# Where the last three columns of the recurrent mixer are taken out of PSUM, and what the bonus sums wait for

## The chip, the cores and the metric

The kernel runs on one core of a Trainium2 chip. The metric is the device time of one launch in microseconds (us). TensorE (PE in the profile) multiplies, VectorE (DVE), ScalarE (ACT) and GpSimd (POOL) work elementwise, SyncE (SP) issues DMAs.

## The reference

The reference is one step of a two-layer decoder trunk over 256 prompt tokens and 8 sequences of 8 sample tokens (320 columns in all). The change sits in the third branch of the mixer, RWKV-7 time mixing:

```
mixed = rwkv_cols + (prev - rwkv_cols) * mu          # token shift over 26 x 128 projected rows
r, kc, vc, wd, ad, gd = split(mixed)
decay = exp(-exp(w_log));  a_lr = sigmoid(a0 + ad @ w_a2)
kk = kc * k_k;  kc = kc * (1 + (a_lr - 1) * k_a);  kk = kk / |kk|
yr, state = rwkv7_scan(r, decay, kc, vc, kk, kk * a_lr, state)
bonus = sum_head(r * kc * r_k) * vc
out_c = (head_norm(yr) * lnx_g + lnx_b + bonus) * g_rw
```

## The kernel before

All activations lie transposed, 128 features by 320 tokens. A weight matrix comes in chunks of 128 by 1024, one for each 128 outputs, and each chunk makes one tile of 128 by 320 in PSUM. For accuracy a chunk is split in a high half (ACT, line 1531) and a low half (POOL line 732 here, DVE line 1944 elsewhere), so TensorE multiplies a chunk in 24 matmuls: 16 with the high half, then 8 with the low half (lines 897, 898 and 901 for the columns of the mixer). SP loads the chunks into a ring of four; a load waits until the chunk four places ahead is multiplied. Four PSUM tiles, gemm_banks, take the results in turn.

The recurrent mixer of a layer runs in four steps.

1. **Columns.** 26 chunks, `rwkv`, numbered c = 0 to 25. DVE takes each tile out of PSUM in `mix_tokens` (lines 2065 to 2070, five instructions) into `mixed`, in the order of ORDER; from then the bank is free (semaphore `psum_free`). Behind that, `prepare_rwkv(c)` does a share of the elementwise preparation of the scan: products of whole tensors of 128x2560 and the eight bonus products r * r_k * kc (128x320 each, line 2117), written into E3, with the mark "rk" behind the eighth. Its last product, kk * a_lr, has the mark "mixed".
2. **Filling chunks.** 15 chunks of `fill_rwkv`, projections that other branches need later, whose results ACT copies to a stage buffer (line 1604) and SP stores to memory. They give TensorE work while DVE ends the preparation. Chunk 0 and 1 go into banks 2 and 3 and wait for 24 columns out of PSUM; chunk 2 and those behind it wait for all 26 and for the filling chunk two before. On TensorE they are lines 946, 947 (high) and 951 (low).
3. **Bonus sums.** Behind four filling chunks, `tile_sums` (line 1016, 10 matmuls of 128x512) sums E3 over each head into mixer_banks and the first tile of gemm_banks. It waits for "rk" and "mixed". Eleven filling chunks follow. DVE waits for the sums (mark "rks"), multiplies them with v (lines 2134 and 2135), sets a state to zero with the mark "done", and scales r and the gate (lines 2149, 2151).
4. **Scan.** It starts on TensorE (line 1052) behind the fifteenth filling chunk and "done".

POOL, in its own order, makes the low halves of the 26 columns and the first four filling chunks, waits for "mixed", issues the store of the shifted columns `sh_out` (line 762), and then makes the low halves of the next 13 chunks, each behind the wait for its high half and for the chunk two before.

Each engine runs its own list in the order written; every DVE instruction of this part is followed by a wait for its own end (`V_`). The marks are semaphores that count up in the order of `pre_v`.

```
if c < 2: pe.wait_ge(psum_free, RING + BASE["rwkv"] + RT - 2)
else:     pe.wait_ge(psum_free, RING + pos - 1)
```

Of the kernel before, what the change touches and what calls it, by code (L numbers as in the profile page):

```python
# [33 lines left out]
KT = D // P  # L34
L = 2
TP = 256
# [11 lines left out]
C64 = 64  # L48
# [46 lines left out]
PREP_FILLS = 15  # L95
XSCALE = float(D // NX) ** -0.5
# [251 lines left out]
def build(nc, ins, outs):  # L348

    with ExitStack() as ctx:  # L350
# [371 lines left out]
        def _(pool):  # L722
# [20 lines left out]
            with pool.Fori(0, L) as l:  # L743
# [17 lines left out]
                pool.wait_ge(pre_v.sem, pre_v.value["mixed"])  # L761
# [106 lines left out]
        def _(pe):  # L868
# [119 lines left out]
            def need(m, name):  # L988
                pe.wait_ge(m.sem, m.value[name])
# [48 lines left out]
            def rwkv():  # L1038
                fill("fill_rwkv", 4)
                need(pre_v, "rk")  # L1040
                need(pre_v, "mixed")
# [880 lines left out]
        def _(dve):  # L1922
# [173 lines left out]
            def prepare_rwkv(c):  # L2096

                (b0, b1), (r0_, r1_), (v0, v1) = sum_spans(), spans(rr), spans(vv)
# [16 lines left out]
                if c == 22:  # L2115
                    for i in range(KT):
                        ins_ = stt(E3[:, i], rr[:, i], PR("r_k", i), kk_[:, i], ALU.mult, ALU.mult)
                        V_(ins_) if i < KT - 1 else V_.mark(ins_, pre_v, "rk")
                if c == 23:
                    ar0, kkc, ec = AR[:, :, 0:NCH, 0], chunks64(Bt[:, :, 0:TP]), chunks64(E[:, :, 0:TP])  # L2120
                    V_(tt(ar0[:, :, :, 1:C64], kkc[:, :, :, 1:C64], ec[:, :, :, 0:C64 - 1], ALU.mult))
                    V_(copy(ar0[:, :, :, 0], kkc[:, :, :, 0]))
                    V_(copy(pend, ec[:, :, :, C64 - 1]))
                if c == 24:
                    ar0 = AR[:, :, NCH, 0].rearrange("p a (b t) -> p a b t", t=SL)
                    kkc, ec = (v[:, :, TP:T].rearrange("p a (b t) -> p a b t", t=SL) for v in (Bt, E))
                    V_(tt(ar0[:, :, :, 1:SL], kkc[:, :, :, 1:SL], ec[:, :, :, 0:SL - 1], ALU.mult))
                    V_(copy(ar0[:, :, :, 0], kkc[:, :, :, 0]))
                    V_(copy(pends, ec[:, :, :, SL - 1]))
                    V_(tt(kk_, kk_, LW, ALU.mult))  # L2130
                if c == RT - 1:
                    V_.mark(tt(Bt, Bt, Aa, ALU.mult), pre_v, "mixed")
                    need(pre_p, "rks")
                    V_(tt(r0_, b0, v0, ALU.mult))
                    V_.mark(tt(r1_, b1, v1, ALU.mult), pre_v, "bonus")
                    arrived(dve, layer, "x_stored")
                    arrived(dve, layer, "shift_stored")
# [557 lines left out]
```

## Time and profile before

| | us |
|---|---|
| runs of the kernel | 3093.7, 3097.57, 3096.59 (median 3096.59) |
| profiled execution: span from first to last instruction | 3101.2 |
| profiled execution: time of its own beside the span | not listed |
| TensorE busy | 2848.1 |
| VectorE busy | 1749.0 |
| ScalarE busy | 1255.2 |
| GpSimd busy | 521.7 |
| mean granted TensorE clock, share of full | 0.955 |

The span is a time of one execution, 4.6 us above the median of the three runs. Busy time says how long an engine was executing, over stages whose limits differ. The timeline of an engine gives, for each instruction, its start, its duration and the idle time ahead of it with what ended it. "x8" after a row means that eight like it follow one another and that the duration is that of all eight. On TensorE the start of the next matmul comes before the end of the last one, since they are pipelined.

### The profile page before, as it was taken

What the parts mean: (1) busy time and instruction counts of PE and PEld (TensorE: products, weight loads), DVE (VectorE), ACT (ScalarE), POOL (GpSimd) and SP (SyncE); (2) the same over time, 40 slices, a digit from 0 to 9 for tenths busy, and PEclk for the clock granted to TensorE, in tenths of its full rate; (3) what the DMA queues carried; (4) which work ended last, traced back from release to release, by engine and by line L of the source; (5) the groups of instructions that cost most, each with busy time, mean ns of one, the idle gap of its engine ahead of it and who ended that gap; (6) DMA issues with size and microseconds to landing.
All of it is one profiled execution on the core that took longest, in us unless ns stands there. A gap on an engine that the chain in (4) does not pass through costs nothing. (4 is left out here: it accounts for less than half of the span.)

```text
span 3101.2 us, 63944 instructions
## 1 busy us (share of the span) xinstructions
PE 2848.1 (92%) x25694; PEld 2651.8 (86%) x25694; DVE 1749.0 (56%) x2611; ACT 1255.2 (40%) x1755; POOL 521.7 (17%) x341
## 2 busy tenths in 40 slices
PE   7998989989989999899989988999798899998997
PEld 7998888877788998799989978987787888977997
DVE  4444764586676665544354457545766766655443
ACT  4534631244332443444254355222543234434542
POOL 0003550054310000000000046400543000000000
PEclk9999989999998999899999999999999999999998
DMA  4444350144374566344344443401454664663443
GB/s 160 150 147 145 109 152 18 29 124 172 98 300 144 180 209 220 130 149 148 116 148 149 147 136 114 130 25 30 127 188 124 251 214 142 220 220 113 149 147 105
DMA packets 119694, 448.21 MB, mean 145 GB/s; under 512 B 13648, under 2 KB 23920, under 8 KB 111664
## 3 DMA queue, kind: packets, MB, share of 16 engines
q1 hardware_dynamic: 97920, 329.78, 33.4%
q0 software_dynamic: 21552, 115.34, 10.1%
q8 instruction: 156, 2.56, 0.3%
q14 instruction: 66, 0.54, 0.1%
HBM read 397.04 MB, written 48.02 MB: 144 GB/s over the span
## 5 line engine op out<-in xcount | busy, mean ns | idle before, releaser
L1531 ACT ACTIVATE w_high<-ring 128x1024 fp32r<-128x1024 f32 x598 | 631.9, 1057 | 746.9 <-PE gemm_banks L901 315.7
L897 PE MATMUL gemm_banks<-in_high,w_high 128*128 128x320 f32 (+1 forms) x2720 | 803.3, 311 | 25.5 <-ACT w_high L1531 13.9
L1944 DVE TENSOR_TENSOR w_low<-ring,w_high 128x1024 fp32r<-128x1024 f32 x436 | 532.5, 1222 | 472.7 <-ACT w_high L1531 472.3
L898 PE MATMUL gemm_banks<-in_low,w_high 128*128 128x320 f32 (+1 forms) x2720 | 795.4, 308 | 0.0
L732 POOL TENSOR_TENSOR w_low<-ring,w_high 128x1024 fp32r<-128x1024 f32 x162 | 414.3, 2566 | 970.9 <-ACT w_high L1531 969.7
L897 PEld LDWEIGHTS gemm_banks<-in_high,w_high 128*128 128x128 f32 x2720 | 515.1, 189 | 32.4 <-issue 14.0
L898 PEld LDWEIGHTS gemm_banks<-in_low,w_high 128*128 128x128 f32 x2720 | 514.9, 189 | 1.7
L901 PE MATMUL gemm_banks<-in_high,w_low 128*128 128x320 f32 (+1 forms) x2720 | 450.8, 308 | 6.3 <-POOL w_low L732 3.8
L901 PEld LDWEIGHTS gemm_banks<-in_high,w_low 128*128 128x128 f32 x2720 | 408.8, 189 | 8.7 <-POOL w_low L732 5.3
L946 PE MATMUL gemm_banks<-in_high,w_high 128*128 128x320 f32 x640 | 208.9, 339 | 22.1 <-DVE arena L2070 16.7
L973 PE MATMUL gemm_banks<-act_high,w_high 128*128 128x320 f32 x704 | 208.2, 308 | 2.5 <-DVE arena L1993 2.5
L974 PE MATMUL gemm_banks<-act_low,w_high 128*128 128x320 f32 x704 | 207.9, 310 | 0.0
L947 PE MATMUL gemm_banks<-in_low,w_high 128*128 128x320 f32 x640 | 199.5, 324 | 0.0
L885 PE MATMUL gemm_banks<-in_high,w_high 128*128 128x320 f32 (+1 forms) x592 | 128.4, 348 | 58.3 <-ACT in_high L1547 53.8
L885 PEld LDWEIGHTS gemm_banks<-in_high,w_high 128*128 128x128 f32 x592 | 97.5, 205 | 84.2 <-issue 45.9
L946 PEld LDWEIGHTS gemm_banks<-in_high,w_high 128*128 128x128 f32 x640 | 128.6, 201 | 43.5 <-issue 31.6
L1604 ACT ACTIVATE stage<-gemm_banks 128x320 f32<-128x320 f32 x80 | 35.0, 437 | 273.4 <-PE gemm_banks L951 255.5
L1052 PE MATMUL gemm_banks<-arena 64*64 64x64 f32 (+1 forms) x2976 | 121.4, 223 | 17.1 <-DVE arena L2172 10.7
L973 PEld LDWEIGHTS gemm_banks<-act_high,w_high 128*128 128x128 f32 x704 | 131.7, 187 | 3.6 <-DVE arena L1993 3.6
L974 PEld LDWEIGHTS gemm_banks<-act_low,w_high 128*128 128x128 f32 x704 | 133.1, 189 | 0.0
L947 PEld LDWEIGHTS gemm_banks<-in_low,w_high 128*128 128x128 f32 x640 | 129.1, 202 | 2.9 <-issue 2.9
L1052 PEld LDWEIGHTS gemm_banks<-arena 64*64 64x64 f32 x2976 | 105.7, 135 | 22.8 <-ACT arena L1726 8.2
(420 smaller groups left out, 4237.4 us busy)
## 6 DMA issues: line engine op xcount, KB each, us to landing
ring<-in_w SPq DMA_DIRECT2D x598, 512.0 KB, 3.6
arena<-in_kc POOLq DMA_DIRECT2D x14, 1024.0 KB, 6.5
arena<-in_vc POOLq DMA_DIRECT2D x14, 1024.0 KB, 7.3
out_fill<-stage SPq DMA_DIRECT2D x80, 160.0 KB, 4.0
arena<-in_ssm POOLq DMA_DIRECT2D x16, 512.0 KB, 13.5
out_s_ssm<-arena POOLq DMA_DIRECT2D x16, 512.0 KB, 13.9
arena<-in_ret POOLq DMA_DIRECT2D x16, 512.0 KB, 22.2
out_s_ret<-arena POOLq DMA_DIRECT2D x16, 512.0 KB, 7.0
```

The costliest lines, as they stand in the source:

```text
L732: nc.gpsimd.tensor_tensor(w_low[:, slot], ring[:, pos % RING, 0:D], w_high[:, slot].bitcast(F32), ALU.subtract).then_inc(weights_split, 1)
L885: mm(dst, w_high[:, slot, w(k)], in_high[:, k, 0:n], start=(k == 0), stop=False)
L897: mm(dst, w_high[:, slot, w(k)], in_high[:, k, 0:n], start=(k == 0), stop=False)
L898: mm(dst, w_high[:, slot, w(k)], in_low[:, k, 0:n], start=False, stop=False)
L901: ins_ = mm(dst, w_low[:, slot, w(k)], in_high[:, k, 0:n], start=False, stop=(k == KT - 1))
L946: mm(dst, w_high[:, slot, w], in_high[:, k], start=(k == 0), stop=False)
L947: mm(dst, w_high[:, slot, w], in_low[:, k], start=False, stop=False)
L973: mm(dst, w_high[:, slot, w], act_high[:, k], start=(k == 0), stop=False)
L974: mm(dst, w_high[:, slot, w], act_low[:, k], start=False, stop=False)
L1052: ins_ = mm(dst[r_], w[r_], src[r_], start=start, stop=stop, skip_group_check=not start)
L1531: f(w_high[:, slot], ring[:, s, 0:D], ACT.Copy).then_inc(weights_high, 1)
L1944: tt(w_low[:, slot], ring[:, pos % RING, 0:D], w_high[:, slot].bitcast(F32), ALU.subtract).then_inc(weights_split, 1)
```

## The change

The eight bonus products are spread over four columns by a table, BONUS_AT: two behind column 22, one behind 23, one behind 24, four behind 25. The products and copies that stood behind columns 23 and 24, and the one behind column 25, go into a new function, `products_rwkv`, which runs behind column 25 and its bonus products. TensorE no longer waits for "mixed" ahead of the bonus sums, only for "rk"; POOL waits for "rk" in the place of "mixed" ahead of the store of `sh_out`. The order of instructions on PE, ACT, POOL and SP stays; only DVE's changes. The names of the marks stay in one order. Line numbers behind line 95 shift by up to 3.

```diff
--- before.py
+++ after.py
@@ -93,6 +93,7 @@
 TOKQ = [0, 1, 8, 7]
 SAVES = 7 + 3 * NS
 PREP_FILLS = 15
+BONUS_AT = {22: (0, 1), 23: (2,), 24: (3,), 25: (4, 5, 6, 7)}
 XSCALE = float(D // NX) ** -0.5
 gate_base = {"ffa13": 0, "ffa2": 0, "ffb13": FT, "ffb2": FT}
 
@@ -758,7 +759,7 @@
                 fill("rwkv", RT // 2, RT)
 
                 fill("fill_rwkv", 0, AHEAD + 2)
-                pool.wait_ge(pre_v.sem, pre_v.value["mixed"])
+                pool.wait_ge(pre_v.sem, pre_v.value["rk"])
                 pool.dma_start(outs["shift"][l], sh_out).then_inc(dma["shift_stored"][0], 16)
                 fill("fill_rwkv", AHEAD + 2, PREP_FILLS + AHEAD)
                 for c in range(NCH):
@@ -1038,7 +1039,6 @@
             def rwkv():
                 fill("fill_rwkv", 4)
                 need(pre_v, "rk")
-                need(pre_v, "mixed")
                 tile_sums(pre_p, "rks", K("bones"), E3)
                 fill("fill_rwkv", PREP_FILLS - 4)
                 need(pre_v, "done")
@@ -2095,7 +2095,6 @@
 
             def prepare_rwkv(c):
 
-                (b0, b1), (r0_, r1_), (v0, v1) = sum_spans(), spans(rr), spans(vv)
                 if c in (16, 18):
                     half = (c - 16) // 2
                     need(pre_p, ("kkss", half))
@@ -2112,29 +2111,31 @@
                 if c == 21:
                     need(pre_a, "norms")
                     V_(tt(Bt, Bt, E3, ALU.mult))
-                if c == 22:
-                    for i in range(KT):
-                        ins_ = stt(E3[:, i], rr[:, i], PR("r_k", i), kk_[:, i], ALU.mult, ALU.mult)
-                        V_(ins_) if i < KT - 1 else V_.mark(ins_, pre_v, "rk")
-                if c == 23:
-                    ar0, kkc, ec = AR[:, :, 0:NCH, 0], chunks64(Bt[:, :, 0:TP]), chunks64(E[:, :, 0:TP])
-                    V_(tt(ar0[:, :, :, 1:C64], kkc[:, :, :, 1:C64], ec[:, :, :, 0:C64 - 1], ALU.mult))
-                    V_(copy(ar0[:, :, :, 0], kkc[:, :, :, 0]))
-                    V_(copy(pend, ec[:, :, :, C64 - 1]))
-                if c == 24:
-                    ar0 = AR[:, :, NCH, 0].rearrange("p a (b t) -> p a b t", t=SL)
-                    kkc, ec = (v[:, :, TP:T].rearrange("p a (b t) -> p a b t", t=SL) for v in (Bt, E))
-                    V_(tt(ar0[:, :, :, 1:SL], kkc[:, :, :, 1:SL], ec[:, :, :, 0:SL - 1], ALU.mult))
-                    V_(copy(ar0[:, :, :, 0], kkc[:, :, :, 0]))
-                    V_(copy(pends, ec[:, :, :, SL - 1]))
-                    V_(tt(kk_, kk_, LW, ALU.mult))
+                for i in BONUS_AT.get(c, ()):
+                    ins_ = stt(E3[:, i], rr[:, i], PR("r_k", i), kk_[:, i], ALU.mult, ALU.mult)
+                    V_(ins_) if i < KT - 1 else V_.mark(ins_, pre_v, "rk")
                 if c == RT - 1:
-                    V_.mark(tt(Bt, Bt, Aa, ALU.mult), pre_v, "mixed")
-                    need(pre_p, "rks")
-                    V_(tt(r0_, b0, v0, ALU.mult))
-                    V_.mark(tt(r1_, b1, v1, ALU.mult), pre_v, "bonus")
-                    arrived(dve, layer, "x_stored")
-                    arrived(dve, layer, "shift_stored")
+                    products_rwkv()
+
+            def products_rwkv():
+
+                (b0, b1), (r0_, r1_), (v0, v1) = sum_spans(), spans(rr), spans(vv)
+                ar0, kkc, ec = AR[:, :, 0:NCH, 0], chunks64(Bt[:, :, 0:TP]), chunks64(E[:, :, 0:TP])
+                V_(tt(ar0[:, :, :, 1:C64], kkc[:, :, :, 1:C64], ec[:, :, :, 0:C64 - 1], ALU.mult))
+                V_(copy(ar0[:, :, :, 0], kkc[:, :, :, 0]))
+                V_(copy(pend, ec[:, :, :, C64 - 1]))
+                ar0 = AR[:, :, NCH, 0].rearrange("p a (b t) -> p a b t", t=SL)
+                kkc, ec = (v[:, :, TP:T].rearrange("p a (b t) -> p a b t", t=SL) for v in (Bt, E))
+                V_(tt(ar0[:, :, :, 1:SL], kkc[:, :, :, 1:SL], ec[:, :, :, 0:SL - 1], ALU.mult))
+                V_(copy(ar0[:, :, :, 0], kkc[:, :, :, 0]))
+                V_(copy(pends, ec[:, :, :, SL - 1]))
+                V_(tt(kk_, kk_, LW, ALU.mult))
+                V_.mark(tt(Bt, Bt, Aa, ALU.mult), pre_v, "mixed")
+                need(pre_p, "rks")
+                V_(tt(r0_, b0, v0, ALU.mult))
+                V_.mark(tt(r1_, b1, v1, ALU.mult), pre_v, "bonus")
+                arrived(dve, layer, "x_stored")
+                arrived(dve, layer, "shift_stored")
 
             def strided(v, *dims, skip=0):
                 return bass.AP(tensor=v.tensor, offset=v.offset + skip, ap=[list(v.ap[0])] + [list(d) for d in dims])
```

DVE behind column 22, before. The row of line 2117 is the bonus products (E3); lines 2065 to 2070 take column 23 out of PSUM; 2121 and 2122 make the first part of AR from Bt and E.

```order
L2117 SCALAR_TENSOR_TENSOR arena<-arena,par 128x320 x8
L2065 TENSOR_SCALAR arena<-gemm_banks,omu 128x320
L2066 SCALAR_TENSOR_TENSOR arena<-gemm_banks,par,arena 128x255
L2068 SCALAR_TENSOR_TENSOR arena<-gemm_banks,par,arena 128x8x7
L2069 SCALAR_TENSOR_TENSOR arena<-gemm_banks,omu,arena 128x8
L2070 TENSOR_SCALAR arena<-gemm_banks 128x9
L2121 TENSOR_TENSOR arena<-arena 128x8x4x63
L2122 COPY arena<-arena 128x8x4
L2123 COPY chunk_decay<-arena 128x32
```

And in the changed kernel, from the same place:

```order
L2115 SCALAR_TENSOR_TENSOR arena<-arena,par 128x320 x2
L2065 TENSOR_SCALAR arena<-gemm_banks,omu 128x320
L2066 SCALAR_TENSOR_TENSOR arena<-gemm_banks,par,arena 128x255
L2068 SCALAR_TENSOR_TENSOR arena<-gemm_banks,par,arena 128x8x7
L2069 SCALAR_TENSOR_TENSOR arena<-gemm_banks,omu,arena 128x8
L2070 TENSOR_SCALAR arena<-gemm_banks 128x9
L2115 SCALAR_TENSOR_TENSOR arena<-arena,par 128x320
```

Two bonus products stand ahead of column 23 in the place of eight, and one behind it where line 2121 and two copies stood.

DVE from the end of column 24 to the bonus, before. Lines 2127 to 2130 are the products of the sample tokens and kk_ * LW, 2132 is Bt * Aa (mark "mixed"), 2134 the product with the bonus sums.

```order
L2070 TENSOR_SCALAR arena<-gemm_banks 128x9
L2127 TENSOR_TENSOR arena<-arena 128x8x8x7
L2128 COPY arena<-arena 128x8x8
L2129 COPY chunk_decay<-arena 128x64
L2130 TENSOR_TENSOR arena<-arena 128x2560
L2065 TENSOR_SCALAR arena<-gemm_banks,omu 128x320
L2066 SCALAR_TENSOR_TENSOR arena<-gemm_banks,par,arena 128x255
L2068 SCALAR_TENSOR_TENSOR arena<-gemm_banks,par,arena 128x8x7
L2069 SCALAR_TENSOR_TENSOR arena<-gemm_banks,omu,arena 128x8
L2070 TENSOR_SCALAR arena<-gemm_banks 128x9
L2132 TENSOR_TENSOR arena<-arena 128x2560
L2134 TENSOR_TENSOR arena<-mixer_banks,arena 128x2048
```

In the changed kernel, from the end of column 25 (its last instruction is the first row):

```order
L2070 TENSOR_SCALAR arena<-gemm_banks 128x9
L2115 SCALAR_TENSOR_TENSOR arena<-arena,par 128x320 x4
L2124 TENSOR_TENSOR arena<-arena 128x8x4x63
L2125 COPY arena<-arena 128x8x4
L2126 COPY chunk_decay<-arena 128x32
L2129 TENSOR_TENSOR arena<-arena 128x8x8x7
L2130 COPY arena<-arena 128x8x8
L2131 COPY chunk_decay<-arena 128x64
L2132 TENSOR_TENSOR arena<-arena 128x2560
L2133 TENSOR_TENSOR arena<-arena 128x2560
L2135 TENSOR_TENSOR arena<-mixer_banks,arena 128x2048
```

All three groups of wide products stand behind column 25 and the last four bonus products, next to one another.

## Rows read from the trace of the kernel before

**Rows 1.** The page: span, and the busy row of TensorE (us, share).
```profile
span 3101.2 us, 63944 instructions
PE 2848.1 (92%) x25694; PEld 2651.8 (86%) x25694; DVE 1749.0 (56%) x2611; ACT 1255.2 (40%) x1755; POOL 521.7 (17%) x341
```

**Rows 2.** Timeline, PE, layer 1: start, us; in brackets idle before and releaser.
```profile
376.85 1.44 PE L901 MATMUL gemm_banks<-in_high,w_low 128*128 128x320 f32 x8 [1.13 <-POOL w_low L732]
...
384.00 1.34 PE L901 MATMUL gemm_banks<-in_high,w_low 128*128 128x320 f32 x8
387.34 0.38 PE L946 MATMUL gemm_banks<-in_high,w_high 128*128 128x320 f32 x1 [2.01 <-DVE arena L2070]
...
402.48 0.61 PE L946 MATMUL gemm_banks<-in_high,w_high 128*128 128x320 f32 x1 [6.33 <-DVE arena L2070]
...
412.33 3.59 PE L1016 MATMUL mixer_banks<-arena,const 128*128 128x512 f32 x8
...
418.96 1.34 PE L951 MATMUL gemm_banks<-in_high,w_low 128*128 128x320 f32 x8
...
454.16 1.34 PE L951 MATMUL gemm_banks<-in_high,w_low 128*128 128x320 f32 x8
```

**Rows 3.** Timeline, PE, layer 2, same columns.
```profile
1920.36 1.33 PE L901 MATMUL gemm_banks<-in_high,w_low 128*128 128x320 f32 x8
...
1938.85 0.60 PE L946 MATMUL gemm_banks<-in_high,w_high 128*128 128x320 f32 x1 [6.33 <-DVE arena L2070]
...
1955.15 1.34 PE L951 MATMUL gemm_banks<-in_high,w_low 128*128 128x320 f32 x8
```

**Rows 4.** Windows, layer 1: length, busy (PE, PEld, DVE, ACT, POOL), PEclk, DMA, GB/s.
```profile
340.00:368.00 28.00, 25.73 (x160) 23.78 (x158) 21.66 (x35) 18.20 (x12) 15.67 (x6) 1.00 0.37 122
...
388.00:390.00 2.00, 2.00 (x10) 2.00 (x9) 2.00 (x1) 0.79 (x1) 0.99 (x1) 0.51 0.96 356
404.00:406.00 2.00, 2.00 (x9) 2.00 (x9) 1.25 (x1) 0.00 (x0) 0.03 (x1) 0.50 0.69 207
```

**Rows 5.** Timeline, DVE, layer 1, from the bonus products to the end of preparation.
```profile
376.36 8.95 DVE L2117 SCALAR_TENSOR_TENSOR arena<-arena,par 128x320 f32<-128x320 f32 x8
...
387.11 4.00 DVE L2121 TENSOR_TENSOR arena<-arena 128x2016 f32<-128x2016 f32 x1
391.14 2.29 DVE L2122 COPY arena<-arena 128x32 f32<-128x32 f32 x1
...
397.29 0.22 DVE L2129 COPY chunk_decay<-arena 128x64 f32<-128x64 f32 x1
...
400.40 0.55 DVE L2065 TENSOR_SCALAR arena<-gemm_banks,omu 128x320 f32<-128x320 f32 x1
...
402.16 0.17 DVE L2070 TENSOR_SCALAR arena<-gemm_banks 128x9 f32<-128x9 f32 x1
402.25 3.01 DVE L2132 TENSOR_TENSOR arena<-arena 128x2560 f32<-128x2560 f32 x1
416.89 2.29 DVE L2134 TENSOR_TENSOR arena<-mixer_banks,arena 128x2048 f32<-128x2048 f32 x1 [11.63 <-PE gemm_banks L1016]
...
439.92 2.19 DVE L2152 MEMSET arena<- 128x2560 f32 x1 [0.60 <-DVE arena L2151]
```

**Rows 6.** Timeline, ACT, layer 1: high halves of the first two filling chunks.
```profile
385.50 1.06 ACT L1531 ACTIVATE w_high<-ring 128x1024 fp32r<-128x1024 f32 x1 [7.07 <-DMA ring<-in_w]
389.21 1.06 ACT L1531 ACTIVATE w_high<-ring 128x1024 fp32r<-128x1024 f32 x1 [2.66 <-DMA ring<-in_w]
```

**Rows 7.** Timeline, POOL, layer 1: low halves beside the columns and filling chunks.
```profile
390.35 3.02 POOL L732 TENSOR_TENSOR w_low<-ring,w_high 128x1024 fp32r<-128x1024 f32 x1 [1.35 <-ACT w_high L1531]
394.12 2.40 POOL L732 TENSOR_TENSOR w_low<-ring,w_high 128x1024 fp32r<-128x1024 f32 x1 [0.76 <-ACT w_high L1531]
397.64 4.93 POOL L732 TENSOR_TENSOR w_low<-ring,w_high 128x1024 fp32r<-128x1024 f32 x1 [1.12 <-ACT w_high L1531]
...
421.79 2.49 POOL L732 TENSOR_TENSOR w_low<-ring,w_high 128x1024 fp32r<-128x1024 f32 x1 [5.47 <-ACT w_high L1531]
```


## The prediction

> **What bounds the kernel now.** I read the page first: TensorE is busy 92% of the span [rows 1], so the time is TensorE's work plus the places where it stands still or runs at the lower clock. Then the waits of TensorE by length: the longest one in the mixer's preparation is the first matmul of a filling chunk behind DVE's line 2070, the last instruction that takes a column out of PSUM. Then the timelines of TensorE, DVE, ACT and POOL around it, and the granted clock by windows.
>
> TensorE's timeline [rows 2] is to be read from the low part of the last column (start 384.00) to the low part of the fifth filling chunk (start 418.96): 34.96 us. What must lie between is five chunks and the bonus sums. A chunk costs 3.52 us: the tenth chunk behind the one of 418.96 starts its low part at 454.16, and 35.20 / 10 = 3.52. Of these, the 16 high matmuls are 3.52 - 1.18 = 2.34 us, as the eight low ones start 1.34 - 0.16 = 1.18 us before the next. The bonus sums start at 412.33 and the high part behind them at 418.96 - 2.34 = 416.62, so they cost 4.29 us. Five chunks and the sums are 17.60 + 4.29 = 21.89 us. The stretch loses **13.07 us**. In layer 2 the same two rows are 1920.36 and 1955.15, 34.79 us apart [rows 3]: a loss of **12.90 us**.
>
> The loss has three parts. The first filling chunk waits 2.01 us for column 23 to leave PSUM, the third waits 6.33 us for column 25 [rows 2], and the rest, 13.07 - 8.34 = 4.73 us, is clock: behind each of the two waits the granted clock is 0.51 and 0.50 of full, the 1.2 GHz level [rows 4].
>
> Why is column 25 late? DVE does the eight bonus products in front of column 23 (8.95 us) and wide products in front of columns 24 and 25; its last instruction for column 25 ends at 402.16 + 0.17 = 402.33 [rows 5]. TensorE had finished that column at 384.00 + 1.34 = 385.34 [rows 2].
>
> **The change, part by part, layer 1.**
>
> *Order on DVE.* The same instructions run, so DVE's own sum is unchanged; what counts is which are in front. Column 23 now has two bonus products in front of it, which start at 376.36 [rows 5]. At the mean of the row, 8.95 / 8 = 1.12 us each, they end at 378.6; if both are among the long ones, some 2 us later. Column 23 was finished at 376.85 + 1.44 = 378.29 [rows 2] and takes 1.85 us to leave PSUM (five instructions, for column 25 from 400.40 to 402.25 [rows 5]). So it is out by 380.5 to 383. Columns 24 and 25 follow as TensorE ends them: column 25 is out at 385.34 + 1.85 = 387.2 in place of 402.3, in the bad case near 390. Either is before the third filling chunk can start, and the 6.33 us go, with the clock that they cost.
>
> *First filling chunk.* What is late next is its own high half: ACT starts it at 385.50 for 1.06 us, behind the weights' DMA [rows 6]. It can start at 386.56, so 1.22 us of 2.01 stay.
>
> *Second filling chunk.* The first ends its matmuls at 386.56 + 3.52 = 390.08, and the second's high half is there at 389.21 + 1.06 = 390.27 [rows 6]: 0.19 us. Its low half took POOL from 390.35 to 393.37 [rows 7] and is wanted at 390.27 + 2.34 = 392.61: 0.76 us.
>
> *Third to sixth.* DVE's wide products now stand beside these chunks without columns between. A low half takes POOL 2.40 or 2.49 us [rows 7] at its usual pace, but 4.93 us in the row of 397.64, which lies over line 2130. The usual low half starts at 421.79, 1.65 us behind the end of the fifth chunk (418.96 + 1.18 = 420.14), and is wanted at 420.14 + 3.52 + 2.34 = 426.00, 4.21 us after its start. At 2.49 us it costs nothing; at 4.93 us TensorE waits 0.72 us. Bounds for the four chunks are 0 and 4 x 0.72 = 2.9 us; I take one such wait, 0.7, because only one of the four low halves of this kind before (390.35, 394.12, 397.64 and the usual one) was that long.
>
> The Trainium skill, "SBUF — State Buffer", section on the two sides of SBUF, says that a GpSimd operation and a DVE operation with two SBUF inputs hold a port pair in turn, each for its whole instruction. By it the worst low half would be one wide product and itself, 3.01 + 2.40 = 5.4 us, and the wait 1.2 us in place of 0.72. The trace agrees in kind: a copy of 128x32 took 2.29 us and one of 128x64 took 0.22 us [rows 5].
>
> *The waits for "mixed".* TensorE now wants only "rk" in front of the sums. "rk" comes at 387.2 + 4 x 1.12 = 391.7 (395 at worst); TensorE reaches the sums at about 402. POOL passes its wait before the low half of the fifth filling chunk, so nothing queued there is held; the store of `sh_out` starts earlier and blocks nothing.
>
> *DVE behind the sums.* From 387.11 to 402.25 + 3.01 = 405.26 DVE was at the wide products and at columns 24 and 25 without a break [rows 5]; 18.15 less 2 x 1.85 us leaves 14.4 us for the wide products, with their contention. They run from 391.7 to about 406.1. The sums now end near 406.5, so DVE starts line 2134 as soon as before relative to TensorE. It needed from 416.89 to 439.92 + 2.19 = 442.1 for all that the scan wants [rows 5], and TensorE is there at 454.16 + 1.18 = 455.3: 13 us of cover stay. If this cover were gone, the scan would start later by what is missing.
>
> **Sum.** Left over in layer 1: 1.22 + 0.19 + 0.76 + 0.7 = 2.9 us. Gained: 13.07 - 2.9 = 10.2 us; layer 2 by the same steps 12.90 - 2.9 = 10.0. Behind the scan's start all is tied to TensorE, so it reaches the end. Against the profiled execution: 3101.2 - 20.2 = 3081.0 us of span. The median of the runs shown lies 4.6 us under that span, so the runs should give 3096.6 - 20.2 = **3076.4 us**.
>
> Bounds of the known case: with only 1.22 + 0.19 left over, 11.6 a layer, 3073.4. With four long waits and the clock at its lower level for one more chunk (below: 2.97 us) and through the first, which adds about 0.65 as it overlaps the wait for the second's low half: 2.17 + 2.9 + 2.97 + 0.65 = 8.7 left, 4.3 gained a layer, 3088. Some 2 us of scatter between runs come on top.
>
> **Rivals.**
>
> *The clock does not come back in full.* Idle times of 1.22, 0.76 and 0.7 us remain within ten us. For it: an idle time of 2.01 was followed by 0.51 [rows 4]. Against: the window 340 to 368 has 28.00 - 25.73 = 2.3 us idle and a clock of 1.00 [rows 4], and the 1.13 us at 376.85 were followed by chunks at full pace. A chunk at the lower level is 408.97 - 402.48 = 6.49 us (to the end of the third, 412.33 + 0.16 - 3.52), 2.97 too many. One or two such chunks a layer leave a gain of 4.3 to 7 us a layer: about 3085 us.
>
> *Slower: POOL and DVE take turns, and the clock stays low.* Place: filling chunks 2 to 8, where the wide products and then lines 2134 to 2152 run beside POOL. If each low half takes 4.93 us, TensorE waits 0.72 us in every chunk, and if the clock falls for these chunks too, each costs 3.69 us. From the third such chunk this eats the 10.2 us. With five: 18.5 - 10.9 (the gain without the wait already counted) = 7.6 us a layer, 3096.6 + 15 = 3112 us. Against it: DVE worked beside POOL from 416.89 to 442.1 before, with a low half of 2.49 us in it [rows 7] and TensorE at 3.52 us a chunk from 418.96 on.
>
> The Trainium skill, "TensorE: Matmul & The Clock Gate", section on PSUM-queue depth-cycling, has a case for it: frequent small idle times between groups of matmuls made the clock swing between its two levels. The trace shows 2.3 us of such idle time from 340 to 368 without a lower clock, so I give it little.
>
> *The gain is taken back at the scan.* If DVE ended its preparation more than 13 us later relative to TensorE, "done" or the zeroed arrays would hold the scan, and the time would be 3094 to 3097. For it: DVE's work is dense from 385 on. Against: the sum above has it on time, with 13 us of cover. The same time would come out if the third chunk were held by something else than `psum_free`; but its low half was ready at 394.12 + 2.40 = 396.5 [rows 7], six us before it was used.
>
> **How the numbers follow.** Forecast 0.76, clock rival 0.13, taken back 0.07, slower 0.04. About 0.2% (6.2 us) is what a measurement of this kernel can tell from no change. Forecast and clock rival are faster by more: 0.89. Taken back is within: 0.07. The predicted time is the likeliest, 3076.4. The range goes from 3071.5 (the upper bound of the gain with scatter) to 3087 (the clock rival and most of the lower bound); it leaves out the last two cases and little of the first.
>
> **What would show it.** Right: the idle time of 6.33 us in front of line 946 gone in both layers; the third filling chunk starting within 10 us of the last column's end (17 before); the clock near 1.00 from 394 on; low part to low part as above 24 to 25 us; "DVE waits for the sums" shorter by about as much as the wide products moved; one or two short waits of line 951 for POOL. Wrong: a clock of 0.5 in that stretch, low halves of 5 us in a row, or an idle TensorE in front of the scan's first matmul.

## The result, and the profile after

| | before | changed |
|---|---|---|
| median of the runs measured side by side, us (six each) | 3096.3 | 3082.18 |
| lowest and highest | 3093.7 to 3099.06 | 3062.27 to 3087.43 |
| profiled execution, span | 3101.2 | 3082.2 |
| profiled execution, its own time | not listed | 3083.83 |
| mean granted clock | 0.955 | 0.958 |

The medians differ by 14.1 us. The ratio of the two kernels' times is given as 0.9943, which is 17.6 us of 3096.3, with a 95% interval of 0.9921 to 0.9965, or 10.8 to 24.5 us: faster, and clear of no change. The forecast was 3076.4 us (20.2 us faster), the range 3071.5 to 3087. The two profiled executions differ by 19.0 us of span.

TensorE's timeline of the changed kernel, layer 1, by start and duration; it answers to [rows 2].

```profile
377.06 1.44 PE L902 MATMUL gemm_banks<-in_high,w_low 128*128 128x320 f32 x8 [1.14 <-POOL w_low L733]
...
384.20 1.34 PE L902 MATMUL gemm_banks<-in_high,w_low 128*128 128x320 f32 x8
386.69 0.41 PE L947 MATMUL gemm_banks<-in_high,w_high 128*128 128x320 f32 x1 [1.16 <-ACT w_high L1531]
...
389.17 1.43 PE L952 MATMUL gemm_banks<-in_high,w_low 128*128 128x320 f32 x8
391.65 0.41 PE L947 MATMUL gemm_banks<-in_high,w_high 128*128 128x320 f32 x1 [1.05 <-ACT w_high L1531]
...
395.79 1.44 PE L952 MATMUL gemm_banks<-in_high,w_low 128*128 128x320 f32 x8 [1.53 <-POOL w_low L733]
397.07 0.31 PE L947 MATMUL gemm_banks<-in_high,w_high 128*128 128x320 f32 x1
...
407.55 1.02 PE L1017 MATMUL gemm_banks<-arena,const 128*128 128x512 f32 x2
410.75 1.33 PE L952 MATMUL gemm_banks<-in_high,w_low 128*128 128x320 f32 x8
...
447.21 0.27 PE L1052 MATMUL mixer_banks<-arena 64*64 64x64 f32 x2
```

The idle time of 6.33 us is gone, and that of 2.01 us has become 1.16. From low part (384.20) to low part (410.75) it is 26.55 us, against 34.96 before: 8.41 us gained. In layer 2 the same rows start at 1914.52 and 1941.08:

```profile
1914.52 1.34 PE L902 MATMUL gemm_banks<-in_high,w_low 128*128 128x320 f32 x8
1917.04 0.42 PE L947 MATMUL gemm_banks<-in_high,w_high 128*128 128x320 f32 x1 [1.18 <-ACT w_high L1531]
...
1921.63 0.41 PE L947 MATMUL gemm_banks<-in_high,w_high 128*128 128x320 f32 x1 [0.68 <-ACT w_high L1531]
...
1926.13 1.44 PE L952 MATMUL gemm_banks<-in_high,w_low 128*128 128x320 f32 x8 [1.89 <-POOL w_low L733]
...
1941.08 1.34 PE L952 MATMUL gemm_banks<-in_high,w_low 128*128 128x320 f32 x8
```

26.56 us, against 34.79: 8.23 gained. Windows of layer 1, with the granted clock in the column behind the five busy times (they answer to [rows 4], columns as there):

```profile
388.00:390.00 2.00, 2.00 (x14) 1.86 (x14) 1.96 (x2) 0.00 (x0) 1.12 (x1) 1.00 0.94 369
394.00:396.00 2.00, 0.47 (x3) 0.21 (x2) 1.97 (x2) 0.00 (x0) 2.00 (x2) 1.00 0.31 121
404.00:408.00 4.00, 4.00 (x12) 1.84 (x12) 3.97 (x2) 1.38 (x2) 4.00 (x2) 1.00 0.77 237
```

The clock is 1.00 where it was 0.51 and 0.50, even in the window that holds the longest idle time left. DVE's timeline of the same stretch answers to [rows 5]:

```profile
387.40 0.17 DVE L2070 TENSOR_SCALAR arena<-gemm_banks 128x9 f32<-128x9 f32 x1
387.48 3.75 DVE L2115 SCALAR_TENSOR_TENSOR arena<-arena,par 128x320 f32<-128x320 f32 x4
391.26 2.26 DVE L2124 TENSOR_TENSOR arena<-arena 128x2016 f32<-128x2016 f32 x1
393.56 2.24 DVE L2125 COPY arena<-arena 128x32 f32<-128x32 f32 x1
395.83 2.31 DVE L2126 COPY chunk_decay<-arena 128x32 f32<-128x32 f32 x1
...
398.84 2.40 DVE L2130 COPY arena<-arena 128x64 f32<-128x64 f32 x1
401.27 0.22 DVE L2131 COPY chunk_decay<-arena 128x64 f32<-128x64 f32 x1
401.52 2.83 DVE L2132 TENSOR_TENSOR arena<-arena 128x2560 f32<-128x2560 f32 x1
404.38 4.86 DVE L2133 TENSOR_TENSOR arena<-arena 128x2560 f32<-128x2560 f32 x1
409.28 2.29 DVE L2135 TENSOR_TENSOR arena<-mixer_banks,arena 128x2048 f32<-128x2048 f32 x1
...
434.80 2.19 DVE L2153 MEMSET arena<- 128x2560 f32 x1 [0.60 <-DVE arena L2152]
448.55 0.42 DVE L2165 TENSOR_TENSOR arena<-mixer_banks,const 128x256 f32<-128x256 f32 x1 [11.55 <-PE mixer_banks L1059]
```

Column 25 is out at 387.57 in place of 402.33. Before line 2135 DVE no longer idles (11.63 us before): the wide products end at 409.24, 0.7 us behind the bonus sums (407.55 + 1.02 = 408.57). ACT's timeline has the high half of the second filling chunk, which answers to the second row of [rows 6]:

```profile
390.54 1.06 ACT L1531 ACTIVATE w_high<-ring 128x1024 fp32r<-128x1024 f32 x1 [3.90 <-DMA ring<-in_w]
```

Last, POOL's timeline, which answers to [rows 7]; the third row is the store of `sh_out`:

```profile
391.68 6.42 POOL L733 TENSOR_TENSOR w_low<-ring,w_high 128x1024 fp32r<-128x1024 f32 x2 [2.56 <-ACT w_high L1531]
398.74 2.41 POOL L733 TENSOR_TENSOR w_low<-ring,w_high 128x1024 fp32r<-128x1024 f32 x1 [0.64 <-ACT w_high L1531]
401.09 0.56 POOL L763 DMA_DIRECT2D out_shift<-arena  x1
402.27 9.26 POOL L733 TENSOR_TENSOR w_low<-ring,w_high 128x1024 fp32r<-128x1024 f32 x2 [0.61 <-ACT w_high L1531]
```

Two low halves in 6.42 us, then two in 9.26 us, where two alone take 4.8. The first of these holds TensorE for 1.53 us; the second pair lies beside the bonus sums, and no wait of TensorE follows it.

### The profile page after: what moved, and what is told of

It reads as the page before. It is cut to its first block and busy times, and to the rows that moved or that the text cites. A ratio compares the mean times of both kernels' runs of the same rounds, so it can differ in the third digit from the quotient of the medians.

```text
span 3082.2 us, 63942 instructions
## 1 busy us (share of the span) xinstructions
PE 2840.6 (92%) x25694; PEld 2642.0 (86%) x25694; DVE 1760.4 (57%) x2611; ACT 1255.6 (41%) x1755; POOL 527.6 (17%) x341
## 5 line engine op out<-in xcount | busy, mean ns | idle before, releaser
L1052 PEld LDWEIGHTS gemm_banks<-arena 64*64 64x64 f32 x2976 | 106.3, 136 | 24.5 <-ACT arena L1726 8.3
## 6 DMA issues: line engine op xcount, KB each, us to landing
out_s_ssm<-arena POOLq DMA_DIRECT2D x16, 512.0 KB, 14.1
```

The costliest lines, as they stand in the source:

```text
L1052: ins_ = mm(dst[r_], w[r_], src[r_], start=start, stop=stop, skip_group_check=not start)
```

## The experiments

**Theory.** What brought the gain is that columns 23 to 25 leave PSUM ahead of the wide products: TensorE stands still less, and it keeps its clock. What lacks to the forecast lies in the first two filling chunks: their loads, and POOL's turn behind line 2124. **Rivals.** The gain comes from the dropped waits for "mixed", and returns to 6.3 us of idle time once they are back; or the difference to the forecast is the scatter of the granted clock elsewhere in the program.

The totals scatter by more than most of these edits are worth, so each kernel is read in two ways: by its total, and by a stretch of its profile, from the first matmul of the last column's low part to the first matmul of the scan. It holds all that the change touches:

| kernel | stretch, layer 1 / layer 2, us | of it at 1.2 GHz | total, median (runs) | ratio to before, 95% |
|---|---|---|---|---|
| before | 71.4 / 71.3 | 13.7 / 10.2 | | |
| changed | 63.0 / 63.0 | 0 / 0 | 3082.2 (6) | 0.9921 to 0.9965 |
| e1, both waits back | 66.3 / 66.5 | 3.4 / 3.4 | 3089.6 (5) | 0.9939 to 0.9982 |
| e2, POOL's wait back | 64.9 / 63.4 | 3.4 / 0 | 3080.1 (4) | 0.9887 to 0.9946 |
| e3, waits alone dropped | 73.2 / 73.2 | 10.2 / 10.2 | 3094.2 (7) | 0.9959 to 0.9993 |
| e4, changed again | 63.1 / 63.1 | 0 / 0 | 3077.0 (4) | 0.9911 to 0.9947 |
| e5, bonus early | 62.1 / 62.2 | 3.4 / 3.4 | 3077.6 (6) | 0.9913 to 0.9962 |
| e6, bonus late | 60.4 / 60.2 | 0 / 0 | 3072.9 (8) | 0.9902 to 0.9948 |
| e7, a low half on DVE | 61.1 / 61.0 | 0 / 0 | 3077.8 (6) | 0.9898 to 0.9967 |
| e8, e7 and loads earlier | 59.2 / 59.2 | 0 / 0 | 3078.3 (6) | 0.9925 to 0.9974 |
| e9, before, TensorE kept busy | 68.7 / 73.3 | 3.4 / 6.8 | 3088.9 (10) | 0.995 to 0.9989 |
| e10, loads earlier | 58.6 / 58.6 | 0 / 0 | 3079.3 (6) | 0.9927 to 0.9968 |
| e11, loads earlier, bonus late | 58.4 / 58.4 | 0 / 0 | 3077.8 (9) | 0.9917 to 0.996 |
| e12, changed, a third time | 63.1 / 61.8 | 0 / 0 | 3082.1 (10) | 0.9932 to 0.9968 |

One more run of e1 took 6958.75 us; why is not known, and it is not counted here (with it the median is 3090.9). Each stretch comes from one profile, so it is one execution's. The changed kernel has three profiles: five of its six stretches are 63.0 or 63.1 us, the sixth 61.8. The kernel before has one, and the part on the waits shows that its stretch can be some 2 us longer.

### The waits

e1 puts both waits for "mixed" back into the changed kernel, e2 POOL's alone, e3 drops TensorE's alone from the kernel before.

```diff
 # e1
-                pool.wait_ge(pre_v.sem, pre_v.value["rk"])
+                pool.wait_ge(pre_v.sem, pre_v.value["mixed"])
...
                 need(pre_v, "rk")
+                need(pre_v, "mixed")
```

> The changed kernel with both waits for mixed put back (TensorE ahead of the bonus sums, POOL ahead of the store of sh_out), the new order on DVE kept. Theory A (the order on DVE frees the columns, and the dropped waits are only needed so that the wide products at the end hold nothing): mixed comes at 409.2 us in layer 1 of the changed kernel and TensorE reaches the sums at 404.4, so TensorE stands still for about 4.8 us a layer, and up to 3 us a layer of lower clock may follow: 10 to 16 us above the changed kernel, near 3094. Rival B (the gain is the dropped waits alone): the whole gain goes, 14 us or a little more, and the idle time of 6.3 us ahead of the third filling chunk would come back, which theory A says stays away.

> The changed kernel with POOL's wait for mixed put back alone. Theory A: POOL passes it at 409.2 us of layer 1, so the low half of the fifth filling chunk is ready near 412.4 and wanted near 411.0: a wait of some 1.4 us and 0.3 at the next, 1.7 us a layer, so 3 to 4 us above the changed kernel. Rival B: POOL's wait is nothing (0 us), the low halves are hidden.

> The kernel before with TensorE's wait for mixed left out and nothing else. Theory A: mixed came at 405.3 us and TensorE reached the sums at 412.3, so nothing waited: within 3 us of the kernel before. Rival B: about 14 us faster.

TensorE's timeline of e1, the second chunk's low part and the bonus sums:

```profile
396.07 2.09 PE L952 MATMUL gemm_banks<-in_high,w_low 128*128 128x320 f32 x8 [1.75 <-POOL w_low L733]
...
407.52 3.67 PE L1017 MATMUL mixer_banks<-arena,const 128*128 128x512 f32 x8 [1.34 <-DVE arena L2134]
```

The wait ahead of the sums is 1.34 us; I had expected 4.8. Two things differ from the changed kernel ahead of both restored waits, so neither is their doing. The low part at 396.07 takes 2.09 us where the changed kernel's takes 1.44: the clock fell behind 1.75 us of idle time, and TensorE came to the sums later. And "mixed" came 2.1 us earlier, counted from the last column's low part, because POOL stood idle when DVE reached the copy below, which took 2.40 us in the changed kernel (398.84):

```profile
399.08 0.23 DVE L2131 COPY arena<-arena 128x64 f32<-128x64 f32 x1
```

What the waits cost is read from the start of the sums. It lies 23.10 us behind the last column's low part (407.52 - 384.42), and 19.92 in the changed kernel (404.12 - 384.20); "mixed" alone sets it, and the lower clock is hidden in the wait. The stretches are 3.3 and 3.5 us longer. So the dropped waits are worth that much a layer here (an estimate with the copy at its 2.40 us is 5), the new order on DVE alone keeps the other 5 us of the gain, and no idle time of 6.3 us returned: that rival is refuted. By its total, e1 lies 12.6 us above e4, the changed kernel measured beside it (10 to 16 expected); the stretches explain 6.6 of that. POOL's timeline of e1:

```profile
399.65 5.04 POOL L733 TENSOR_TENSOR w_low<-ring,w_high 128x1024 fp32r<-128x1024 f32 x1 [1.31 <-ACT w_high L1532]
408.09 0.56 POOL L763 DMA_DIRECT2D out_shift<-arena  x1 [3.40 <-DVE arena L2134]
```

"mixed" is there at 407.4, while the changed kernel's line 2133 ends at 409.24.

e2 has the same 3.40 us wait on POOL in layer 1 and 6.76 us in layer 2, and no wait of TensorE for POOL follows from it. Its stretch is longer by 1.9 us in layer 1, with 3.4 us at the lower clock, and by 0.4 in layer 2, without. That lower clock begins at 396.39, ahead of POOL's wait, so it is not the wait's doing, and 0.4 us is less than the 1.3 by which the changed kernel's own stretches differ. The 1.7 us a layer that I had expected for POOL's wait did not show; e2's total is 3.1 us above e4's (3 to 4 expected), which the scatter covers.

e3 is no gain in its stretch: 1.8 and 1.9 us longer than before. Its DVE timeline shows why; the copy of line 2122 took 0.2 us in the kernel before:

```profile
391.90 2.29 DVE L2121 COPY arena<-arena 128x32 f32<-128x32 f32 x1
394.23 2.28 DVE L2122 COPY chunk_decay<-arena 128x32 f32<-128x32 f32 x1
```

Column 25 is out 2.2 us later (20.57 us behind the last column's low part, 18.33 before), and the wait of TensorE's third chunk rises to 9.79 us. The edit, which comes behind the columns in every list, did not do this. In e3 the clock did not fall behind the first wait (2.01 and 2.04 us), so the first filling chunk ended sooner, POOL began the third chunk's low half sooner (9.39 us behind the last column's low part, 10.12 before), and the copy fell into it. Layer 2 of e9 below has the same instructions up to there and does the same; so the kernel before can lose these 2 us as well. Its profile caught the shorter case in both layers, and the gain of a layer may be 10 us and not 8.4 where it is the longer one.

In the stretch, then, the waits for "mixed" cost nothing while the columns are late, and dropping them pays only with the new order. e3's total is still 6.2 us below the kernel before beside it, with an interval wholly below 1, where I had expected 3 us at most. Its runs had a higher mean granted clock (0.959 against 0.957), and its profile has 265 us at 1.2 GHz in the whole program against 278; what raised it outside the stretch is open.

### The order of the bonus products

e5 puts all eight bonus products behind column 22, as before, with the wide products still last (POOL waits for the columns in place of "rk"). e6 puts all eight behind column 25.

```diff
-BONUS_AT = {22: (0, 1), 23: (2,), 24: (3,), 25: (4, 5, 6, 7)}
+BONUS_AT = {22: (0, 1, 2, 3, 4, 5, 6, 7)}    # e5
+BONUS_AT = {25: (0, 1, 2, 3, 4, 5, 6, 7)}    # e6
```

> The changed kernel with all eight bonus products behind column 22, as before the change; the wide products stay last and the dropped waits stay dropped. As rk now comes before the last column is out, POOL waits for all 26 columns out of PSUM instead. The measure is the stretch from the first matmul of the last column's low part to the first matmul of the scan in the profile (71.4 us a layer before, 63.0 in the changed kernel). Theory A (what held the third filling chunk were the wide products between the columns; the spread of the bonus products matters little): column 23 is out at 387.2, the first filling chunk waits 2.0 in place of 1.16 us, columns 24 and 25 are out by 391, before the third chunk: stretch 63.8, or 65.5 if the clock falls behind the 2 us; 2 to 5 us above the changed kernel in all. Rival E (the spread is what frees the columns): the 6.3 us come back, stretch near 71, 3095 or more.

> The changed kernel with all eight bonus products behind column 25. Theory A: the columns leave PSUM as they come, rk comes near 396 us where the sums want it at 404, DVE ends the wide products some 4 us later and still has about 8 us of cover ahead of the scan; the second filling chunk's low half now meets bonus products of 0.55 us and not a wide product, so its wait may shrink: stretch 62 to 63 us. Rival F (DVE's own list is close to setting the start of the scan): TensorE waits at the sums or at the scan, stretch 65 or more.

TensorE's timeline of e5:

```profile
386.73 0.39 PE L947 MATMUL gemm_banks<-in_high,w_high 128*128 128x320 f32 x1 [2.01 <-DVE arena L2070]
...
390.70 1.33 PE L952 MATMUL gemm_banks<-in_high,w_low 128*128 128x320 f32 x8
...
394.21 1.34 PE L952 MATMUL gemm_banks<-in_high,w_low 128*128 128x320 f32 x8
```

The wait of 2.01 us for column 23 is back, and with it 3.4 us of the lower clock. Still the stretch is 0.9 us shorter than the changed kernel's (62.1 us where 63.8 to 65.5 was expected), because the next two waits are gone: the high halves were ready by then, and POOL began the second low half at 389.80, ahead of line 2124 (390.09), and made it in 2.40 us; it was line 2124 that waited in turn, 4.22 us in place of 2.26, and nobody waits for that. So the spread of the bonus products over four columns is worth nothing in this stretch; the place of the wide products is what frees the columns.

e6 is shorter by 2.6 to 2.8 us a layer than the changed kernel (62 to 63 us expected, 60.4 and 60.2 measured). Its second chunk starts without a wait, and its low part too. Part of this is that the second chunk's load landed earlier, so that its high half began at 389.26 in place of 390.54 (see the loads below). The rest is POOL: beside the eight bonus products it makes two low halves in 5.21 us, not 6.42. This row of its POOL timeline stands against the first one of the changed kernel:

```profile
390.39 5.21 POOL L733 TENSOR_TENSOR w_low<-ring,w_high 128x1024 fp32r<-128x1024 f32 x2 [1.19 <-ACT w_high L1531]
```

### What is left in the first two chunks

e7 gives the second filling chunk's low half to DVE, between "rk" and the wide products. e10 and e11 issue the loads of the first filling chunks earlier: the two empty places of the ring that followed the columns (segment "pad3") move behind the filling chunks, and the counts and ring slots with them; e11 also has e6's order. e8 is e7 and e10 together. Of e10's edit only the line with the places is shown.

```diff
 # e7, POOL
-                fill("fill_rwkv", 0, AHEAD + 2)
+                fill("fill_rwkv", 0, 1)
+                pool.wait_ge(weights_split, RANK[BASE["fill_rwkv"] + 1] + 1)
+                fill("fill_rwkv", 2, AHEAD + 2)
 # e7, DVE, ahead of products_rwkv()
+                    dve.wait_ge(weights_split, RANK[BASE["fill_rwkv"]] + 1)
+                    weights(0, RING, BASE["fill_rwkv"] + 1)
 # e10
-SEGS = [("ffa13", 2 * FT), ("ffa2", FT), ("pad2", 2), ("rwkv", RT), ("pad3", 2), ("fill_rwkv", 20), ("ssm", 1 + CB), ("pad", 3),
+SEGS = [("ffa13", 2 * FT), ("ffa2", FT), ("pad2", 2), ("rwkv", RT), ("fill_rwkv", 20), ("pad3", 2), ("ssm", 1 + CB), ("pad", 3),
```

> The changed kernel with one low half moved: DVE makes that of the second filling chunk, right behind rk and ahead of the wide products (1.22 us as in its other low halves), and POOL goes on with the third. Theory G (what is left of the loss beyond the forecast, 1.5 us in layer 1 and 1.9 in layer 2 ahead of this low part, is POOL waiting for its turn behind DVE): both idle times vanish, stretch near 61.4 us, 3 us below the changed kernel. Rival H (the low half is late since its high half is late, whoever makes it): stretch unchanged near 63.

> As the kernel before this one, and the two empty positions of the ring between the columns and the filling chunks are moved behind the filling chunks, so that the loads of the first two filling chunks wait for columns 22 and 23 and no longer for 24 and 25. Theory I (the 1.16 and 1.05 us ahead of the first two filling chunks are the weights' DMA): they go as well, stretch near 59.3 us, 7 us below the changed kernel in all, near 3072. Rival J (something else is as late, such as column 23 or the slot of the high half): idle times stay near 1 us, stretch 61.

> The changed kernel with the two empty positions of the ring moved behind the filling chunks and nothing else, so the loads of the first two filling chunks start two columns earlier. Theory I: the 1.16 and 1.05 us ahead of these chunks go, stretch 60.8 us; POOL's wait for its turn (1.5 to 1.9 us) stays at one of the chunks. Rival L (POOL's late low half moves with the chunk and hides what is gained): stretch near 63.

> Both edits that shortened the stretch without a new wait: the empty positions moved and all eight bonus products behind column 25. If they add (2.2 and 2.7 us of the changed kernel's 63.0): stretch 58.5 to 59 us, close to the least that five chunks and the sums allow (57.9 from 63.0 less all idle time and the 1.2 of stalls hidden in it). Total: 8 us below the changed kernel if the rest of the program holds, which the scatter of single runs by 10 us and more lets be seen only as a tendency.

DVE's timeline of e7:

```profile
391.01 1.23 DVE L1946 TENSOR_TENSOR w_low<-ring,w_high 128x1024 fp32r<-128x1024 f32 x1 [0.41 <-ACT w_high L1533]
```

DVE makes the low half in 1.23 us, the second low part starts without a wait, and the stretch is 61.1 and 61.0 us, as expected (61.4): the 1.53 us were POOL's turn. With the loads earlier as well, e8 has no idle time in the first two chunks, 0.54 us ahead of the third's low part, and a stretch of 59.2 us, as expected (59.3). Its total (3078.3) did not come down to the 3072 that I expected.

e10 was better than expected: 58.6 against 60.8. TensorE's timeline of e10, low parts of the first three filling chunks:

```profile
387.12 1.34 PE L954 MATMUL gemm_banks<-in_high,w_low 128*128 128x320 f32 x8
...
390.64 1.34 PE L954 MATMUL gemm_banks<-in_high,w_low 128*128 128x320 f32 x8
...
394.29 1.45 PE L954 MATMUL gemm_banks<-in_high,w_low 128*128 128x320 f32 x8
```

3.52 us and 3.65 us apart: the chunks run at the floor of 3.52 us, all but 0.13. POOL's slow pair of 6.63 us is still there, but one chunk further on, where it is nearly hidden, so e7's edit is not needed once the loads are early. e11 goes to the floor of the prediction: 21.89 us from the last column's low part to the fifth chunk's, and no idle time. Its total is 4.3 us below e12, the changed kernel beside it, where 8 was expected.

The loads of the first two filling chunks are ordered alike in all kernels without e10's edit, and the second one still lands early or late. In the changed kernel, e1, e2, e4, e7 and e12 its high half begins 5.95 to 6.34 us behind the last column's low part, in the kernel before, e3, e5, e6 and e9 5.0 to 5.3 us. One thing on record goes with it: in the twelve late stretches a packet of the queue that carries instructions falls into these loads, 4.0 to 4.4 us behind the low part, and in the ten early ones it is missing or falls at another time. The DMA view of the changed kernel from 388 to 389 us has it; that of e6 has none:

```profile
q14 instruction: 1, 0.01, 1.9%
```

That the packet holds up the load is not shown; no run moves it alone.

### The clock

e9 takes the kernel before and leaves its waits as they are, but puts 42 matmuls, whose product is not used, into TensorE's idle time behind the second filling chunk.

```diff
-                fill("fill_rwkv", 4)
+                fill("fill_rwkv", 2)
+                for k in range(42):
+                    mm(bank(1)[:, 0:T], in_high[:, k % KT, 0:P], in_high[:, k % KT], start=True, stop=True)
+                fill("fill_rwkv", 2)
```

> The kernel before with 42 matmuls added between the second and the third filling chunk, where TensorE waits 6.3 us for the last column: high half of the input times itself, 128x320 each, into a mixer bank that is free there; nobody reads the result. At 0.147 us each they fill 6.2 us. Forecast's reckoning (of the 13 us lost in this stretch 4.7 are the lower clock behind the two waits, near 3 of them in the third filling chunk): the stretch from the last column's low part to the scan goes from 71.4 to about 68.4 us, although the wait for the column stays, and the clock is 1.00 behind it; total 3 to 9 us below the kernel before. Rival K (the third chunk is slow for another reason, such as its weights coming in): stretch 71 us, the chunk still takes 6.5 us.

TensorE's timeline of e9, layer 1:

```profile
395.40 6.32 PE L1041 MATMUL mixer_banks<-in_high 128*128 128x320 f32 x42
401.93 0.39 PE L946 MATMUL gemm_banks<-in_high,w_high 128*128 128x320 f32 x1 [0.21 <-DVE arena L2073]
...
404.35 1.34 PE L951 MATMUL gemm_banks<-in_high,w_low 128*128 128x320 f32 x8
```

And its window behind the wait:

```profile
402.00:406.00 4.00, 4.00 (x28) 4.00 (x29) 2.76 (x1) 0.28 (x1) 0.60 (x2) 1.00 0.74 206
```

The third chunk starts as late as before (18.5 us behind the last column's low part), but its high part takes 404.35 - 401.93 = 2.42 us at a clock of 1.00; before, at 0.50, it took 4.40. The stretch of layer 1 is 68.7 us, 2.7 less than before (expected 68.4), with no wait shorter. This is the clock's share behind the long wait, by itself, in one layer of one run. In layer 2 the copy of line 2126 took 2.31 us in place of 0.2, column 25 left 2.3 us later than in layer 1, and TensorE stood still for another 3.73 us behind the 42 matmuls. The stretch is 73.3 us: there the run shows nothing of the clock. The total is 8.0 us below the kernel before beside it (3 to 9 expected), but the two stretches together are 0.7 us shorter, so it does not bear the forecast out.

### The changed kernel again

e4 and e12 are the changed kernel, with no edit.

> The changed kernel itself, unchanged, in the same call. Its runs so far went from 3062 to 3087 us where the kernel before kept to 3094 to 3099. Theory C (idle times at other places of the program are long enough that the granted clock falls after them or not, as they fall in time): runs again spread by over 10 us, and time and mean granted clock go together, about 3 us for 0.001 of the clock. Rival D (the one fast run was a fault of that launch): all runs within 5 us of 3083.

> The changed kernel once more, in one call with the kernel before and with more rounds. Forecast: 17 us below the kernel before by the two stretches (8.4 us each), plus or minus what the clock elsewhere gives; so a ratio of 0.993 to 0.996, stretch 63.0 us again in both layers.

e4's runs lie 7 us apart (3075.3 to 3082.32), those of the kernel before beside them 13 us: neither the 10 us and more of theory C nor the 5 us around 3083 of rival D. e12 lies 14.8 us below the kernel before, with a ratio of 0.995 as expected. Its stretch is 63.1 us in layer 1, but 61.8 in layer 2: there POOL began the second low half 0.16 us ahead of line 2124 and had the first turn. Over all that was measured, the changed kernel has a median of 3080.6 us (20 runs, 3062.3 to 3090.1) and the kernel before 3096.0 (61 runs, 3083.2 to 3111.9): 15.4 us. Within either kernel the time follows the mean granted clock of the run, some 2.2 to 2.6 us less for each 0.001 more. The profile of e4 has 234 us at 1.2 GHz in the whole program, that of the changed kernel 258, with stretches that are alike to 0.2 us. A total is thus moved by several us from outside the stretch, and the last rival holds in part: not for the stretch, whose loss is measured, but for what the totals lie above or below it.

## Why the prediction was right

By its steps, layer 1:

- **Order on DVE: right.** Column 25 out at 387.2 forecast, 387.57 measured; "rk" at 391.7 forecast, 391.2 measured. The 6.33 us went in both layers.
- **The clock came back in full: right.** 1.00 in all windows of the stretch, against the rival with 0.13; e9 shows the term by itself, in layer 1. It was close: in e1, in layer 1 of e2 and in e5 it fell for 3.4 us.
- **What is left over: mis-sized.** This is the step that made the forecast too large. It was 1.22 + 0.19 + 0.76 + 0.7 = 2.9 us. By starts in TensorE's timeline it is: the first chunk 386.69 - 384.20 - 1.18 = 1.31, and 0.14 until its low part; the second's high half 391.65 - 389.17 - 1.18 = 1.30; its low half 395.79 - 391.65 - 2.34 = 1.80, and 0.10 behind it. The sum is 4.65 us, which is all of 26.55 - 21.89 = 4.66. Two of my own signs show it: the third chunk starts 397.07 - 385.54 = 11.5 us behind the last column's end, where I wanted 10, and low part to low part is 26.55 us, where I wanted 24 to 25.
- *Second chunk's high half, 0.19 forecast, 1.30 measured.* I took its time from [rows 6], 389.21; in the changed kernel ACT starts it at 390.54, when its load has landed. e10, with the loads earlier, has no such wait. Why this load landed later is open, but for the packet that goes with it; layer 2 has an idle time of 0.68 us there, layer 1 1.05.
- *Its low half, 0.76 forecast, 1.80 measured.* I kept the 3.02 us that POOL took beside other work. Now POOL's turn came behind line 2124 (391.26 to 393.52), so the low half was ready 4.1 us after 391.68. I had priced a lost turn only for the chunks behind, and it fell on this one; e7, which takes the low half from POOL, shows it.
- *One long low half in the third to sixth, 0.7 forecast, nothing measured.* This came out at nothing for a reason that I did not have: the pair of 9.26 us was long, but it fell beside the bonus sums, which need no weights, 4.29 us of cover that I had not counted. By my reckoning it would have cost more than 0.7.
- **DVE's wide products: 14.4 us forecast, 391.26 to 409.24 = 18.0 measured,** since three small copies waited for POOL's turn (2.24, 2.31, 2.40 us; one before) and line 2133 took 4.86 in place of 3.01. The end of the preparation is at 434.80 + 2.19 = 437.0 and the scan starts at 447.2: 10.2 us of cover against 13 forecast. It was enough, by a margin that hid the error.
- **The slower rival (0.04)** had POOL and DVE take turns in each of chunks 2 to 8. The turns came, and two low halves in a row took 9.26 us, nearly the 5 us each that I had named as a sign of being wrong; but they held no matmul, and the clock stayed.

The gain of the stretches is 8.4 + 8.2 = 16.6 us, in place of 20.2. The medians show 14.1 and the ratio 17.6, with an interval from 10.8 to 24.5, which holds all of them; what lies between them is not resolved. So the mechanism is right, and the size is too large by 3.6 us of the stretches. That the median fell into the range proves little: I had allowed some 2 us of scatter between runs, and the six runs went from 3062.3 to 3087.4.

**A version that beats both?** In the stretch e11 is best, 4.6 us a layer less than the changed kernel's 63.0, and e6, a change of one line, takes 2.7. Their totals, 3077.8 and 3072.9, lie below the changed kernel's 3080.6, but e10 and e11, better than e6 by their stretches, have no better totals. That either beats the changed kernel is shown for the stretch, not for the whole.

## What to carry to other kernels

When an engine both empties the buffers of a producer and prepares other work, let it empty first, and put the long operations last: with the waits behind it dropped, that took 8.3 us of waiting and some 4.7 us of clock from each layer and left 4.7 us of smaller losses, while spreading the short products gave nothing. A wait is worth dropping only once what stands ahead of it no longer hides it. A moved order needs new arrival times for everything that was "just in time": the two terms that I had taken over from the old trace, the second chunk's high half and its low half, were the ones that were wrong. Where totals scatter by more than the edit is worth, compare a stretch between two fixed instructions.

## What the runs showed of the hardware

A DVE copy of 128x32 or 128x64 took 0.20 to 0.23 us, or 2.2 to 2.4 us when a subtraction of POOL was under way, in every run here, and which of the two it was changed from run to run of nearly the same order. This alone moved column 25 by some 2.2 us in e3 and in layer 2 of e9. POOL's low half in turn took 2.40 us alone and over 4 us behind a wide product of DVE. The operations that read PSUM (lines 2065 to 2070) kept their durations throughout. The Trainium skill, "SBUF — State Buffer", section on the two sides of SBUF, says that the one who comes second waits for the whole instruction of the other; these durations agree, down to the copies.

Idle times of 1.05 to 1.53 us within ten us left the granted clock at 1.00 in the changed kernel, and so did one of 1.89 in layer 2; behind 1.75 us in e1 and 2.01 in e5 it was lower for 3.4 us. The length of an idle time alone did not decide it: in e2 the clock fell behind 1.88 us in layer 1 and stayed behind 1.90 in layer 2, and in e3 it stayed behind 2.01 and 2.04.
